# Attention core of a float32 block: where the multiplication by the values and its result stand among the steps of a stage

## The reference

```python
def block_attention(q, k, v, scale):
    def one_block(qi):                       # 128 queries at a time
        s = jnp.einsum("bqhgd,bkhd->bhgqk", _f32(qi), kf) * scale
        p = jax.nn.softmax(s, axis=-1)       # over 1280 keys: 256 of the context, 1024 of the sequence
        return jnp.einsum("bhgqk,bkhe->bqhge", p, vf)
o_a = block_attention(q_a, k_a, v_a, GQA_HEAD_DIM ** -0.5)
o_m = block_attention(q_m, k_m, v_m, (MLA_NOPE_DIM + MLA_ROPE_DIM) ** -0.5)
y = (jnp.concatenate([o_a, o_m], axis=-1) * jax.nn.silu(gate)) @ w_out
```

## Time and profile before

| what | us |
|---|---|
| median of 3 runs (lowest, highest) | 5220.36 (5216.55, 5220.53) |
| the profiled execution, its own time | 5216.07 |
| its span, first to last instruction | 5214.3 |
| TensorE busy, whole span | 4836.2 (93%) |
| VectorE busy, whole span | 1997.6 (38%) |
| ScalarE busy, whole span | 988.1 (19%) |

### The profile page before, as it was taken

One profiled execution on the slowest core, in us unless ns is written; L12 is line 12 of the kernel. 1 busy time (PEld: TensorE's weight loads), 2 busy tenths in 40 slices (PEclk: granted clock), 3 DMA queues, 4 the chain that ended last, 5 costly groups with the idle time before them and its releaser, 6 DMA issues.

```text
span 5214.3 us, 40015 instructions
## 1 busy us (share of the span) xinstructions
PE 4836.2 (93%) x16966; PEld 2373.9 (46%) x16966; DVE 1997.6 (38%) x2340; ACT 988.1 (19%) x1318; POOL 3.9 (0%) x7
## 2 busy tenths in 40 slices
PE   7989999996999988889888898999999999999998
PEld 3446565542444434344455444444444444444443
DVE  3445555313333366563454544423511124333102
ACT  1134444202111100001333232222200000000000
POOL 0000000000000000000000000000000000000000
PEclk8999999997999999999999999999999999999999
DMA  5100000112232322222000001112221111111211
GB/s 234 60 29 1 1 1 1 45 39 110 89 105 94 140 89 111 93 113 74 33 21 22 25 33 41 37 41 77 83 89 39 36 63 49 41 46 43 72 40 51
DMA packets 85693, 313.95 MB, mean 60 GB/s; under 512 B 9061, under 2 KB 27237, under 8 KB 77450
## 3 DMA queue, kind: packets, MB, share of 16 engines
q1 hardware_dynamic: 68156, 293.57, 15.6%
q10 hardware_dynamic: 17360, 17.83, 1.0%
HBM read 254.22 MB, written 57.15 MB: 60 GB/s over the span
## 4 chain that ended last, share of the span: by engine, by line
PE 64%; DVE 9%; issue 2%; ACT 2%; DMA 0%; DVEq 0%; SPq 0%; ACTq 0%
PE late_dense L115 40%; PE late_four L2787 6%; PE late_two L2787 3%; PE late_four L1023 3%; PE late_four L1241 1%; PE late_four L2022 1%; PE late_two L1320 1%; PE late_two L1312 1%; PE late_four L1040 1%; PE late_four L1035 1%; DVE late_arena L2232 1%; PE late_two L1258 1%; PE late_two L2345 0%; PE late_two L2347 0%; PE late_two L2048 0%
## 5 line engine op out<-in xcount | busy, mean ns | idle before, releaser
L115 PE MATMUL late_dense<-late_arena 128*128 128x512 f32 x5416 | 2378.8, 599 | 24.7 <-DVE late_arena L2705 10.0
L115 PEld LDWEIGHTS late_dense<-late_arena 128*128 128x128 f32 x5416 | 1035.1, 192 | 1313.5 <-issue 1301.8
L128 ACT ACTIVATE late_arena<-late_dense 128x512 f32<-128x512 f32 x226 | 134.8, 597 | 1396.3 <-PE late_dense L115 1383.3
L2787 PE MATMUL late_four<-late_arena 128*128 128x512 f32 x752 | 326.6, 592 | 0.0
L115 PE MATMUL attn_dense<-attn_h,attn_wbuf 128*128 128x512 f32 x576 | 253.3, 598 | 7.6 <-DVE attn_h L551 6.6
L2787 PEld LDWEIGHTS late_four<-late_arena 128*128 128x128 f32 x752 | 142.9, 190 | 179.8 <-issue 176.7
L659 PE MATMUL attn_dense<-matrices,attn_work 128*128 128x128 f32 x1280 | 193.9, 282 | 32.0 <-ACT attn_work L707 15.8
L2705 DVE TENSOR_TENSOR late_arena<-late_dense,late_arena 128x512 f32<-128x512 f32 x64 | 44.2, 691 | 420.1 <-PE late_dense L115 420.1
L2022 PE MATMUL late_four<-late_arena 128*128 128x128 f32 (+1 forms) x1024 | 119.4, 318 | 84.9 <-DVE late_arena L2165 54.5
L1023 PE MATMUL late_four<-late_arena 128*128 128x512 f32 x384 | 171.5, 600 | 9.7 <-DVE late_arena L1057 6.6
L659 PEld LDWEIGHTS attn_dense<-matrices,attn_work 128*128 128x128 f32 x1280 | 135.2, 140 | 92.5 <-issue 58.8
(11 more groups left out here) (374 smaller groups left out, 4889.2 us busy)
## 6 DMA issues: line engine op xcount, KB each, us to landing
attn_q<-in_ada_w SPq DMA_DIRECT2D x12, 2048.0 KB, 9.5
late_arena<-in_w_ffn_in SPq DMA_DIRECT2D x44, 512.0 KB, 4.2
late_arena<-in_hy_tables SPq DMA_DIRECT2D x16, 1280.0 KB, 6.1
late_arena<-in_hy_w_in SPq DMA_DIRECT2D x32, 512.0 KB, 3.5
spectrum<-late_arena SPq DMA_DIRECT2D x8, 2048.0 KB, 8.5
late_arena<-spectrum SPq DMA_DIRECT2D x8, 2048.0 KB, 12.5
late_arena<-in_w_gates SPq DMA_DIRECT2D x32, 512.0 KB, 3.4
late_arena<-x SPq DMA_DIRECT2D x6, 2048.0 KB, 10.2
```

What stands on the lines that cost most here:

```text
L115: mm = pe.matmul(self.ps[:, n % SEG], self.wbuf[:, slot, k], job.rhs[:, k, cols], start=(job.first and k == 0), stop=(job.last and k == kt ...
L128: act.activation(job.out[:, cols], self.ps[:, n % SEG], job.func, scale=job.scale, bias=job.bias).then_inc(self.emptied[n % SEG], 1)
L2787: mm = pe.matmul(product_bank(M, name, i), left[:, k], right[:, k], start=(k == 0), stop=(k == 3))
```

## The change

weigh(s-1) is taken out of the middle of the transposes and put right behind scores(s+1). The five groups follow it in one row. The banks alternate now: T0, T2 and T4 use bank 0, T1 and T3 and weigh use bank 1. T1 is the group that waits for `stored`. keep(s-1) moves on VectorE from behind copy 2 to between max(s+1,0) and max(s+1,1). In the last turn, which has no maxima, it stands ahead of copy 2. ScalarE's list of steps is the same as before; only the banks that its copies read change. No instruction is added or removed.

```diff
 def turn_group_pe(pe, Y, s, j):
-    bank = Y.banks[j % 2] if j < 3 else Y.banks[(j + 1) % 2]
+    bank = Y.banks[j % 2]
...
     if s or j >= 2:
-        if j in (0, 2, 3):
-            pe.wait_ge(Y.copied[0], 3 * s + (0, 0, 1, 2)[j])
-        elif j == 1:
-            pe.wait_ge(Y.copied[1], 2 * s)
-        else:
-            pe.wait_ge(Y.copied[1], 2 * s + 1)
-            if s:
-                pe.wait_ge(Y.stored, s)
+        pe.wait_ge(Y.copied[j % 2], (3, 2)[j % 2] * s + j // 2)
+    if s and j == 1:
+        pe.wait_ge(Y.stored, s)
...
 def weigh_pe(pe, Y, s):
-    pe.wait_ge(Y.copied[1], 2 * (s + 1) + (1 if s + 1 < STAGES else 0))
+    pe.wait_ge(Y.copied[1], 2 * (s + 1))
     pe.wait_ge(Y.copied[0], 3 * (s + 1))
...
 def core_pe(pe, Y):
             scores_pe(pe, Y, s + 1)
-        for j in range(3):
-            turn_group_pe(pe, Y, s, j)
         if s:
             weigh_pe(pe, Y, s - 1)
-        for j in (3, 4):
+        for j in range(5):
             turn_group_pe(pe, Y, s, j)
...
 def copy_group(Y, s, j):
-    bank = Y.banks[j % 2] if j < 3 else Y.banks[(j + 1) % 2]
-    return Y.turned[:, s % 2, 4 * j:4 * j + 4], bank.rearrange("p (k c) -> p k c", c=P), Y.copied[0 if j in (0, 2, 3) else 1]
+    return Y.turned[:, s % 2, 4 * j:4 * j + 4], Y.banks[j % 2].rearrange("p (k c) -> p k c", c=P), Y.copied[j % 2]
...
     def maximum(s):
         for e in range(2):
+            if e and s >= 2:
+                keep(s - 2)
...
         if s + 1 < STAGES:
             maximum(s + 1)
+        else:
+            keep(s - 1)
         copy(s, 2)
-        if s:
-            keep(s - 1)
         copy(s, 4)
```

## The result

| | before | after |
|---|---|---|
| median (lowest, highest), us | 5220.44 (5216.55, 5223.42) | 5372.38 (5368.82, 5380.93) |
| the profiled execution, its own time | 5216.07 | 5380.93 |
| its span | 5214.3 | 5379.1 |
| mean granted clock over the span | 0.961 | 0.948 |

The ratio of the executions is 1.0294, with a 95% interval of 1.0276 to 1.0312. The kernel is slower by 152 us in the medians. The forecast was slower by 90 (5310), with a range that ended at 5334. The sign and the longer stage were right; the clock, which was put at nothing, was not.

A forecast was written before the change was run, and what follows sets the result against it. TensorE was taken to set the pace, with the exponentials having 1.1 us of slack per stage. 62 x 1.48 = 91.8 us on 5216.07 gave 5307.9; a median between 5308 and 5312 was expected, stated as 5310, range 5296 to 5334.

The forecast's parts named there:

- steps 1 to 6: New order of one stage, worked out engine by engine: period 9.75 for 8.27 us, +1.48; latent 12.90 for 11.42.
- B: Start of the scores: TensorE's own order binds, not the exponentials; +0.25 a stage, +16 us, 5232; chance 0.04.
- C: Each stage: ScalarE's idle time absorbs later copies, so TensorE runs without its waits; 53 us less, 5163; chance 0.04.
- D: Each stage: the change acts less than worked out, within 0.2% of before, 5220; chance 0.02.
- The bound of 112 us: Turns 1 to 62: upper end of the 89 to 112 us added, from 1.43 to 1.8 us a stage.
- So I expect it to stay: TensorE's clock in the core: stays at 1.00 although TensorE stands 1.1 us in one piece per stage.
- rival A: From weigh's end to the next scores: clock falls; if every other stage, 155 us, in all 5463; chance 0.05.

The follow-up runs named there:

- e1: Changed kernel with exp 0 of the next stage put ahead of copy 0 and copy 1 on ScalarE; 5251.51 us, ratio to before 1.0064.
- e5: Changed kernel with weigh's result in free columns of a score bank, so no transposes wait for keep; 5291.34 us, ratio to before 1.0138.
- e3: Changed kernel with 8 filler transposes of the identity behind T4 in each stage; 5315.77 us, ratio to before 1.0183.
- e8: Changed kernel with 4 filler transposes of the identity behind T4 in each stage; 5313.35 us, ratio to before 1.018.
- e2: Changed kernel with 8 filler matmuls, identity by identity, behind T4 in each stage; 5347.29 us.
- e6: Changed kernel with keep put back behind both maxima, weigh still behind the scores; 5358.85 us, ratio to before 1.0297.
- e4: Kernel before, with the spreading of shares moved from weigh to between T1 and T2 and its copy between the maxima; 5187.94 us, ratio 0.994.
- keep alone: Kernel before, with only keep moved between the maxima and weigh still between T2 and T3; 5488.35 us, ratio 1.0517.

## Why the prediction was right or wrong

**The order at full clock: right.** The steps 1 to 6 gave 9.75 and 12.90, and the stages took 9.80 and 12.95. Counted from the stage's start, weigh was forecast to start at 2.35 (it started at 2.35), T1 at 5.79 (5.78), exp 0 at 6.96 (6.94), the last read-out to end at 9.68 (9.66). The release of the scores was a little under: I took 0.05 to 0.10 and it took 0.14. TensorE stood 1.27 us ahead of the scores where 1.1 was forecast. e1 and e5 confirm the parts: 0.98 of the increment goes when exp 0 no longer stands behind the copies, and 0.36 goes when T1 no longer waits for keep. Rivals B and C, which needed the scores to follow T4 at once, fell with the 1.27 us released by the exponential; D, no change, fell with the period of 9.80.

**The sum at full clock: right.** 62 x 1.48 = 91.8 us was forecast. Without the falls, e3 and e8 took 5315.8 and 5313.4, 94 us above before, inside the stated range. The bound of 112 us was not needed.

**The clock: wrong, and the whole of the miss.** The step that failed is the paragraph that ends "So I expect it to stay": it put the clock at nothing in the sum, and the runs showed 66.7 us for it in the profiled execution and some 57 in the medians. With it failed the chance and the price of rival A. I took two rows for evidence, transposes alone at 1.00 and a fall behind a long stretch of nothing, and looked at each part of the new stage by itself. The new stage puts both in a row: a block of transposes with small waits between them, and then 1.28 us of standing, which gave 1.81 busy of 3.40 us. The row that I relied on had 2.92 of 3.40. It was no row for this case, and the trace of before had nearer ones that I had not brought in, one of them 20 us ahead of the core. One with the same busy time, behind which the clock stayed, and one with less, behind which it was at 0.50:

```profile
2605.90:2609.30 3.40, 1.82 (x11) 1.34 (x12) 0.00 (x0) 2.21 (x3) 0.00 (x0) 1.00 0.00 0
2609.30:2612.70 3.40, 3.40 (x9) 1.50 (x8) 0.00 (x0) 0.34 (x1) 0.00 (x0) 1.00 0.00 0
325.80:329.20 3.40, 1.48 (x5) 0.56 (x4) 3.25 (x3) 0.00 (x0) 0.00 (x0) 1.00 0.00 0
329.20:332.60 3.40, 3.40 (x7) 1.67 (x6) 1.23 (x1) 0.64 (x1) 0.00 (x0) 0.50 0.00 0
```

They show that the clock could fall behind a stretch in which TensorE was not idle throughout, and 5 chances in 100 for rival A did not respect that. They do not tell which stage falls. The same stretch ahead of the scores of another stage of the changed kernel looks the same as the one ahead of the fall, and the stage behind it, the first one shown above, ran at full clock:

```profile
566.49:569.89 3.40, 1.80 (x12) 1.17 (x12) 1.93 (x5) 3.40 (x6) 0.00 (x0) 1.00 0.00 0
```

A had the right place and the wrong reason. It said "the clock falls in the stretch of transposes and waiting", for the transposes' sake; e3 added transposes to this very stretch and ended the falls. Its comparison with the fall at 356.5 was misread too: TensorE had stood there for 4.89 us, so the new stretch of 4.8 us is not longer. It priced a fall at 5.0 us in every other stage, 155 us; the profiled execution lost 66.7 us in 15 stages, 4.4 us each, and most executions a little less, about 57 (5372.4 against 5315.8). The measured median lies 38 us above the end of the range.

The rule of the Trainium skill (TensorE: Matmul & The Clock Gate, Part 4: PE-mode transpose), that transposes do not count as activity in the same way, is not borne out if it is read as "not at all": with 8 transposes in the pause all stages ran at 1.00. Whether they count for less than other matmuls, no run here shows: e2 and e3, with ordinary matmuls and with transposes in the pause, both kept the clock.

**What stays open.** Why e6, with longer pauses than the changed kernel, lost the clock in one stage only. The length of the pause ahead of the scores does not order the falls: 0.74 us (e8) and 0.91 (e5) had none, 1.28 (the changed kernel) had 15, 1.52 (e6) had one. e6 has another period (10.38 against 9.80), so its pauses may lie otherwise in time; one of its executions lost some 48 us more than the others. That is an argument, and no run here shows it.

## What to carry to other kernels

When a step is moved ahead on the bounding engine, follow the queues of the engines that are idle: an idle engine with a fixed order is no slack, and a step whose input is long ready can be stuck behind one that has just been made late. Between two urgent steps put only work whose input is already there (the copy of e4, 34 us gained), never work that has to be waited for (keep alone, 268 us lost). And if a change makes TensorE stand once a stage, do not take the clock as given from one row: look for rows at either level behind light work, give the fall a price and a real chance, and fill the pause as a test.

## What the runs showed of the hardware

- A pause of 1.28 us behind five groups of transposes, repeated each stage, cost the full clock in 15 of 61 stages; a fall lasted up to 13.6 us although TensorE was busy all through it. With 16 transposes put ahead of the first turn, none of the turns hit was one that was hit without them. Pauses of 0.74 us (e8) and 0.91 us (e5) did no harm in any of 61 stages.
- Work that nobody reads made the kernel faster: 8 transposes a stage, 57 us (e3 against the changed kernel).
- A float32 matmul of 128 x 128 by 128 columns ran as two instructions and took about twice as long as a transpose of the same size (0.11 us from start to start, and as much for each of the two instructions), so 8 of them held up the scores by 0.58 us.
